# Feed-forward up projections of a two-layer decoder: 18 of 22 column blocks by seven block products, activations kept in three portions

## What is computed

```
y = x * rsqrt(mean(x*x) + 1e-6) * gain
g, u = split(y @ w_gu, 2)            # w_gu: 1024 x (2 * 2816)
x = x + 0.5 * (silu(g) * u) @ w_down # w_down: 2816 x 1024
```

## Time and profile before

| | us |
|---|---|
| median of three runs (2206.16 to 2210.08) | 2208.39 |
| the profiled execution, its own time | 2211.56 |
| its span, first to last instruction | 2209.9 |
| mean granted TensorE clock, share of full | 0.989 |

### The profile page before, as it was taken

The page is one execution under the profiler, slowest core; times in us unless marked ns, Lnnn a source line. Parts: engine busy times, 40 slices in busy tenths (PEclk is TensorE's granted clock), DMA queues, the critical chain, the costliest instruction groups (busy, mean ns, idle before and its releaser), DMA issues.

```text
span 2209.9 us, 32685 instructions
## 1 busy us (share of the span) xinstructions
PE 2150.4 (97%) x12778; PEld 1748.2 (79%) x12778; DVE 1116.6 (51%) x1335; ACT 756.9 (34%) x997; POOL 373.5 (17%) x376
## 2 busy tenths in 40 slices
PE   7999999998988999999999999999999999999998
PEld 6888888776887888888877888887667688888887
DVE  4443445666855544344574433446665654434464
ACT  5432222353323342222353422223444443322234
POOL 2000003444541200000330000013333310000032
PEclk9999999998999999999999999999999999999999
DMA  5324322321002433333243323324323243243232
GB/s 153 95 77 113 95 76 86 87 67 38 4 4 59 124 95 88 103 96 85 88 117 91 90 86 109 95 77 115 86 76 87 65 120 99 78 113 95 74 88 86
DMA packets 365441, 192.35 MB, mean 87 GB/s; under 512 B 10015, under 2 KB 362385, under 8 KB 365345
## 3 DMA queue, kind: packets, MB, share of 16 engines
q1 hardware_dynamic: 363104, 185.10, 29.9%
q0 software_dynamic: 2224, 5.86, 0.9%
q10 hardware_dynamic: 16, 0.00, 0.0%
HBM read 188.81 MB, written 2.13 MB: 86 GB/s over the span
## 4 chain that ended last, share of the span: by engine, by line
PE 91%; DVE 4%; ACT 2%; issue 2%; POOL 1%; DMA 0%; SPq 0%; POOLq 0%; DVEq 0%; ACTq 0%
PE bank L420 25%; PE bank L422 25%; PE bank L421 25%; PE bank L1469 2%; PE bank L2114 2%; PE bank L2116 2%; PE bank L2115 2%; PE bank L831 1%; PE bank L832 1%; PE bank L833 1%; PE bank L2131 1%; PE bank L2150 1%; PE bank L2161 1%; DVE w_lo L410 1%; ACT w_hi L405 0%
## 5 line engine op out<-in xcount | busy, mean ns | idle before, releaser
L420 PE MATMUL bank<-xn_hi,w_hi 128*128 128x512 f32 x1416 | 555.0, 392 | 10.6 <-DVE w_lo L2618 5.8
L421 PE MATMUL bank<-xn_hi,w_lo 128*128 128x512 f32 x1416 | 552.6, 390 | 0.0
L422 PE MATMUL bank<-xn_lo,w_hi 128*128 128x512 f32 x1416 | 552.4, 390 | 0.0
L405 ACT CAST w_hi<-w_raw 128x2048 fp32r<-128x2048 f32 (+3 forms) x209 | 325.7, 1558 | 641.4 <-PE bank L422 560.0
L410 DVE TENSOR_TENSOR w_lo<-w_raw,w_hi 128x2048 fp32r<-128x2048 f32 (+3 forms) x207 | 423.7, 2047 | 148.0 <-ACT w_hi L405 147.2
L420 PEld LDWEIGHTS bank<-xn_hi,w_hi 128*128 128x128 f32 x1416 | 266.7, 188 | 69.2 <-DVE w_lo L2618 6.0
L421 PEld LDWEIGHTS bank<-xn_hi,w_lo 128*128 128x128 f32 x1416 | 266.8, 188 | 56.3 <-issue 1.0
L422 PEld LDWEIGHTS bank<-xn_lo,w_hi 128*128 128x128 f32 x1416 | 266.9, 188 | 55.7
L422 PE MATMUL bank<-h_lo,w_hi 128*128 128x512 f32 x704 | 273.9, 389 | 0.0
L420 PE MATMUL bank<-h_hi,w_hi 128*128 128x512 f32 x704 | 273.9, 389 | 0.0
L421 PE MATMUL bank<-h_hi,w_lo 128*128 128x512 f32 x704 | 273.9, 389 | 0.0
(11 more groups left out here) (337 smaller groups left out, 2682.5 us busy)
## 6 DMA issues: line engine op xcount, KB each, us to landing
w_raw<-in_ffn_w_gu_dram SPq DMA_DIRECT2D x176, 512.0 KB, 5.0
w_raw<-in_ffn_w_down_dram SPq DMA_DIRECT2D x64, 384.0 KB, 3.9
w_raw<-in_ffn_w_down_dram SPq DMA_DIRECT2D x64, 320.0 KB, 3.6
w_raw<-in_even_w_in_dram SPq DMA_DIRECT2D x40, 256.0 KB, 3.3
w_raw<-in_ple_w_gate_dram SPq DMA_DIRECT2D x16, 512.0 KB, 3.8
w_raw<-in_fox_w_in_dram SPq DMA_DIRECT2D x16, 512.0 KB, 4.8
w_raw<-in_even_w_out_dram SPq DMA_DIRECT2D x16, 256.0 KB, 3.3
w_raw<-in_fox_w_in_dram SPq DMA_DIRECT2D x16, 256.0 KB, 4.1
```

The source lines that it names most:

```text
L405: nc.scalar.copy(w_hi[slot][:, 0:tiles], w_raw[slot][:, 0:tiles]).then_inc(w_hi_ready, 1)
L420: nc.tensor.matmul(dst, w[0], hi[:, k], start=k == 0, stop=False)
L421: nc.tensor.matmul(dst, w[1], hi[:, k], start=False, stop=False)
L422: last = nc.tensor.matmul(dst, w[0], lo[:, k], start=False, stop=k == tiles - 1)
```

## The change

**Seven products for eight.** An up job is a product of a matrix of weights, cut into 2x2 pieces (the two halves of the output, gate and other, by the two halves of the 1024 channels), with a matrix of activations, cut into 2x2 pieces (channels 0 to 511 and 512 to 1023, tokens 0 to 255 and 256 to 511). In place of the eight products of pieces the new job makes seven, with sums of pieces as operands (Winograd's arrangement). Each product has 4 blocks of channels, 3 matmuls each, with 256 columns in place of 512: 84 matmuls of 128x256 for 48 of 128x512. It is used for 18 of the 22 up jobs of each feed-forward block, 72 in all; the first 4 (CLASSIC) run as before, and the activation sums are made meanwhile.

**The sums.** Per job GpSimd makes four 128x512 sums or differences of weight pieces (`ffn_pool`; one of them in place in w_raw, three into the single buffer sums), ScalarE rounds those three (`split_sums_hi`, 128x1536) and VectorE makes their low part (`split_sums_lo`). GpSimd starts on the next job only when the low part of the last sums is made (`s_ready`). Per feed-forward block VectorE multiplies x by gain and rinv (`scale_all`, 8 instructions), GpSimd makes four 128x1024 differences of the result, and both, with three 128x1024 pieces of the scaled activations themselves, are split again (`t_his`, `t_los`, `b_hi`, `b_lo`).

**Putting together.** The seven results go to halves of banks; ScalarE copies one (p1, 128x256) and VectorE combines them in five instructions (u2, u4_u3 and three writes to gu). Silu and the product now follow from gu, and the rounding of a job's result stands in the next job.

**Portions.** CHUNKS = (8, 7, 7) takes the place of (12, 10): three sets of up jobs and three sets of 8 down jobs, over 8, 7 and 7 blocks. The up jobs of the first portion are written out, of the others the first is. The core of the diff:

```diff
-HALVES = (12, 10)
+CHUNKS = (8, 7, 7)
+CLASSIC = 4
+T_ORDER = (0, 2, 1, 3)
...
+        p1, u2 = rinv[:, 0:T // 2], rinv[:, T // 2:T]
+        u4_u3 = other
+        at(SCRATCH)
+        gu = view("gu", [P, 2 * T])
+        at(SCRATCH + 8)
+        sums = view("sums", [P, 12, P])
...
-        def each_job(e, name, step, peel_first=False):
+        def each_job(e, name, step, lead=0):
 
 
 
             base, count = jobs.phases[name]
-            lead = 2 if peel_first else 0
             for j in range(lead):
                 step(base + j, j, (base + j) % 2, jobs.of(base + j + 2))
+            if lead == count:
+                return
...
+                    if not isinstance(j, int) or j >= (CLASSIC + 2 if c == 0 else 2):
+                        e.wait_ge(s_ready, seven(st, c, j) - 1)
...
+        def ffn_pool(pool, st):
+            norm, i = norms[st], ffn_index[st]
+            left, right = slice(0, T // 2), slice(T // 2, T)
+
+            def difference(dst, plus, minus):
+                nc.gpsimd.tensor_tensor(t_sum[:, dst], plus, minus, ALU.subtract).then_inc(t_made, 1)
+
+            pool.wait_ge(scaled_made, DT * i + DT // 2)
+            difference(0, scaled_k1[:, :, right], scaled_k1[:, :, left])
+            pool.wait_ge(scaled_made, DT * i + DT)
+            difference(2, scaled_k2[:, :, right], scaled_k1[:, :, right])
+            pool.wait_ge(t_made, 4 * i + 1)
+            difference(1, scaled_k2[:, :, right], t_sum[:, 0])
+            pool.wait_ge(t_made, 4 * i + 3)
+            difference(3, scaled_k2[:, :, left], t_sum[:, 1])
+
+            for c, tiles, h0 in chunks(st):
+                def up(n, j, slot, _):
+                    if classic(c, j):
+                        return
+                    f = seven(st, c, j)
+                    w = w_raw[slot]
+                    pool.wait_ge(w_loaded[slot], loads_due(n, slot))
+                    if not isinstance(j, int) or (c, j) != (0, CLASSIC):
+                        pool.wait_ge(s_ready, f)
+                    nc.gpsimd.tensor_tensor(sums[:, 0:4], w[:, 8:12], w[:, 12:16], ALU.add).then_inc(sums_made, 1)
+                    pool.wait_ge(sums_made, f * 4 + 1)
+                    nc.gpsimd.tensor_tensor(w[:, 8:12], w[:, 0:4], w[:, 8:12], ALU.subtract).then_inc(sums_made, 1)
+                    nc.gpsimd.tensor_tensor(sums[:, 4:8], sums[:, 0:4], w[:, 0:4], ALU.subtract).then_inc(sums_made, 1)
+                    pool.wait_ge(sums_made, f * 4 + 3)
+                    nc.gpsimd.tensor_tensor(sums[:, 8:12], w[:, 4:8], sums[:, 4:8], ALU.subtract).then_inc(sums_made, 1)
+                each_job(pool, f"{st}up{c}", up, tiles if c == 0 else 3)
...
+            def of_seven(dst, w, b):
+                for k in range(4):
+                    nc.tensor.matmul(dst, w[0][:, k], b[0][:, k], start=k == 0, stop=False)
+                    nc.tensor.matmul(dst, w[1][:, k], b[0][:, k], start=False, stop=False)
+                    last = nc.tensor.matmul(dst, w[0][:, k], b[1][:, k], start=False, stop=k == 3)
+                return last
...
+                    pe.wait_ge(w_ready, n + 1)
+                    pe.wait_ge(s_ready, f + 1)
+                    pe.wait_ge(banks_free, n - 1)
+                    if first:
+                        pe.wait_ge(t_ready, 4 * i + 4)
+                    of_seven(bank[2 * slot][:, left], s(0), t(0))
+                    of_seven(bank[2 * slot][:, right], w(8), t(2)).then_inc(parts_done, 1)
+                    if first:
+                        pe.wait_ge(b_ready, 3 * i + 1)
+                    if f_before(f):
+                        pe.wait_ge(u2_made, f)
+                    of_seven(bank[5][:, left], w(0), b(0, left))
+                    of_seven(bank[5][:, right], s(1), t(1)).then_inc(parts_done, 1)
+                    if first:
+                        pe.wait_ge(b_ready, 3 * i + 2)
+                        pe.wait_ge(banks_free, n)
+                    if f_before(f):
+                        pe.wait_ge(c12_made, f)
+                    of_seven(bank[1][:, left], s(2), b(1, right))
+                    of_seven(bank[1][:, right], w(12), t(3)).then_inc(parts_done, 1)
+                    if first:
+                        pe.wait_ge(b_ready, 3 * i + 3)
+                    else:
+                        pe.wait_ge(act_in_ready, j + (g0 + sum(CHUNKS[:c])))
+                    of_seven(bank[3][:, left], w(4), b(1, left)).then_inc(job_done, 1)
+                each_job(pe, f"{st}up{c}", up, tiles if c == 0 else 1)
...
+                def up_classic(n, j, slot, ahead):
+                    act.wait_ge(job_done, n + 1)
+                    if j == CLASSIC - 1:
+                        b_hi(0, scaled_k1, left)
+                        b_hi(1, scaled_k2, right)
+                        gate(j)
+                        split_seven_hi(n + 2, seven(st, c, j + 2), slot)
+                        b_hi(1, scaled_k2, left)
+                        return
+                    if classic(c, j + 2):
+                        split_hi(act, n + 2, slot, ahead)
+                    else:
+                        split_seven_hi(n + 2, seven(st, c, j + 2), slot)
+                    gate(j)
+                    if not classic(c, j + 2):
+                        split_sums_hi(seven(st, c, j + 2), slot)
+                    h_high(j, prod)
+                    if j == 1:
+                        t_his()
...
+                    nc.scalar.copy(p1[:], bank[5][:, left]).then_inc(p1_copied, 1)
+                    if first:
+                        split_sums_hi(f + 1, 1 - slot)
+                        h_high(j - 1, prod)
+
+                    def gate_seven():
+                        act.wait_ge(act_in_ready, j + (g + 1))
+                        act.wait_ge(c12_made, f + 1)
+                        nc.scalar.activation(bank[4][:], gu[:, 0:T], ACT.Silu).then_inc(act_out_ready, 1)
+
                     act.wait_ge(job_done, n + 1)
-                    split_hi(act, n + 2, slot, ahead)
-                    act.wait_ge(act_in_ready, j + (g0 + 1))
-                    nc.scalar.activation(act_out[:], act_in[:], ACT.Silu).then_inc(act_out_ready, 1)
-                    act.wait_ge(prod_ready, j + (h0 + 1))
-                    nc.scalar.copy(h_hi[:, ds(j)], prod[:]).then_inc(h_hi_ready, 1)
-                each_job(act, f"{st}up{half}", up)
-                g0 += tiles
-                h0 += tiles
+                    if last:
+                        gate_seven()
+                        split_hi(act, n + 2, slot, ahead)
+                    elif isinstance(j, int) and j + 2 == tiles:
+                        split_hi(act, n + 2, slot, ahead)
+                        gate_seven()
+                    else:
+                        split_seven_hi(n + 2, f + 2, slot)
+                        gate_seven()
+                        split_sums_hi(f + 2, slot)
+                    h_high(j, bank[6])
+                each_job(act, f"{st}up{c}", up, tiles if c == 0 else 1)
...
+                    if to_up and j == DT - 2:
+                        split_sums_hi(f, slot)
                     act.wait_ge(job_done, n + 1)
-                    split_hi(act, n + 2, slot, ahead)
-                each_job(act, f"{st}down{half}", down)
+                    if to_up:
+                        split_seven_hi(n + 2, f, slot)
+                    else:
+                        split_hi(act, n + 2, slot, ahead)
+                    if to_up and j == DT - 1:
+                        split_sums_hi(f, slot)
+                each_job(act, f"{st}down{c}", down)
...
+                    if first:
+                        b_lo(0, scaled_k1, left, 1)
+                        classic_prod(n - 1, j - 1)
+                        b_lo(1, scaled_k2, right, 2)
+                        split_lo(dve, n + 1, 1 - slot, 2 * DT)
+                        b_lo(1, scaled_k2, left, 3)
+                        split_sums_lo(f + 1, 1 - slot)
+                        dve.wait_ge(prod_ready, j + h0)
+                    dve.wait_ge(p1_copied, f + 1)
+                    nc.vector.tensor_tensor(u2[:], bank[5][:, right], p1[:], ALU.add).then_inc(u2_made, 1)
+                    dve.wait_ge(u2_made, f + 1)
+                    nc.vector.tensor_tensor(halves(u4_u3[:]), halves(bank[2 * slot][:]),
+                                            u2[:].rearrange("p (o t) -> p o t", o=1).broadcast_to([P, 2, T // 2]),
+                                            ALU.add).then_inc(u34_made, 1)
+                    if not begins:
+                        h_low(j - 1, prod if first else bank[6])
+                    dve.wait_ge(u34_made, f + 1)
+                    nc.vector.tensor_tensor(gu[:, T + T // 2:], bank[2 * slot][:, left], u4_u3[:, right],
+                                            ALU.add).then_inc(banks_free, 1)
+                    dve.wait_ge(parts_done, f * 3 + 3)
+                    nc.vector.tensor_tensor(gu[:, T // 2:T + T // 2], bank[1][:], u4_u3[:],
```

(30 more changed lines are left out.)

215 lines of the change are left out of this document (168 added, 47 removed).

## The result

The changed kernel takes 2237.43 us (median of 4 runs, 2233.67 to 2238.28) against 2208.15 for the kernel before. The ratio is 1.013, with a 95% interval from 1.0117 to 1.0143: slower, as forecast, by 29 us where I had 16. The profiled execution's span is 2236.4 us, 26.5 more than before.

What follows compares the result with a forecast made beforehand. TensorE's matmul count and spacing were taken to bound the feed-forward blocks. Terms of - 63 + 51 + 23 + 5 = + 16 us on the median of 2208.4 gave 2224, range 2174 to 2266 (the forecast's own 2213 to 2242).

Steps and rivals of the forecast that it cites:

- Part 1: Matmuls of the 72 new up jobs: 84 narrow ones, 0.1201 us apart or 0.1134; jobs of 10.0 us, 63 us won.
- Part 2: New up jobs: GpSimd's sums and VectorE's work form a loop through the single sums buffer, 10.1 us a job.
- The loop of 10.1 us: New up jobs: two GpSimd sums, ScalarE's rounding, then VectorE's wait, w_lo, product and low part of the sums.
- rival (a): New up jobs: narrow matmuls 0.1134 us apart, loop 9.4, jobs 9.53; 2170 to 2190 us, chance 0.29.
- Part 3: Down to up borders, twice a block: pauses of 3.9 and 5.7 us plus half clock; 12.8 a block, 51 in all.
- Part 4: From old up jobs to new ones: VectorE late with operands, 5.7 us a block, 23 in all.
- I take a pause of 2.4: Before each block's first new job: VectorE's work with port waits takes 35.2 us, TensorE wants it at 32.6.
- Part 5: Up to down borders and the last portion's down jobs: small waits, 1.2 us a block, 5 in all.
- (b): New up jobs: narrow matmuls 0.127 us apart, only 15 us won; 2272 us, chance 0.07.
- (c): New up jobs: GpSimd and VectorE contend for the SBUF port, loop 11.2 us; 2287 us, chance 0.07.
- (d): New up jobs: weight loads and streams add up, 18.3 us a job; 2821 us, chance 0.01.
- (e): Whole kernel: pauses and gain cancel, 2204 to 2213 us, chance 0.11.

Runs made afterwards that it cites:

- Experiment 9: Kernel before, with down-job matmuls cut in columns (four of 128 in the first portion, 384 and 128 in the second), each with its own weight load: 2986.75 us.
- experiment 8: Changed kernel with GpSimd's four weight sums of each job cut to one column, except in each block's first new job (results wrong): 2193.79 us.
- Experiment 2: Changed kernel with weights split before sums for the first up job of the second and third portions: 2214.07 us, ratio 1.0034.
- experiment 7: Changed kernel with five old up jobs a block and VectorE's four t_lo split in two pairs over two jobs: 2210.72 us, ratio 1.0013.
- Experiments 3: Changed kernel with five old up jobs ahead of the new ones in each block, in place of four: 2223.97 us, ratio 1.0075.
- experiment 1: Kernel before, with portions of 8, 7 and 7 in place of 12 and 10, all up jobs as before: 2221.48 us, ratio 1.007.

## Why the prediction came out as it did

**Part 1, right, its size 5 us too good.** The spacing is 0.120, the candidate with a fixed 0.0134 us on 256 columns. Experiment 9 has a third point: 384 columns at 0.173 = 0.160 + 0.013. The forecast took 10.0 us a job, from between 9.53 and 10.1; measured 10.08, 57.6 won and not 63.

The Trainium skill's rule (TensorE: Matmul & The Clock Gate, Part 3, What overlaps and what doesn't), by which loads of the same rows would add to the streams, is not borne out by any run: 0.120 for 256 columns, 0.173 for 384.

**Part 2, right in that GpSimd's work hinders VectorE, wrong in what follows.** The loop of 10.1 us set the pace nowhere but in the two jobs behind the first new one, for 0.2 us a block: TensorE, at 10.08, has no gap in a steady row of jobs, and without the sums (experiment 8) such a row is no faster. How close the loop is can be read in the second portion of the first block, where VectorE's s_lo does not wait for TensorE:

```profile
178.40 1.74 DVE L800 TENSOR_TENSOR s_lo<-sums,s_hi 128x1536 fp32r<-128x1536 f32 x1
...
188.26 1.74 DVE L800 TENSOR_TENSOR s_lo<-sums,s_hi 128x1536 fp32r<-128x1536 f32 x1
```

The loop takes 9.86 us, 0.2 less than TensorE's job, and over five jobs s_lo's lead over TensorE grows from 1.1 to 1.9. A job faster than 9.86, as rival (a) has it, would have needed a shorter loop as well. The port is worse than I had priced it: three VectorE instructions in one job lost 4.9 us, and GpSimd's own are 1.75 to 2.28 beside VectorE's.

The Trainium skill (GPSIMD Engine Reference, Specifications) has VectorE's instructions with two SBUF inputs in contention with GpSimd for the shared interfaces. The trace agrees, with 2.88 us for 0.69; `other`, with one SBUF input, kept its 0.67.

**Part 3, right.** Pauses of 3.9 and 5.7 were forecast, 2.8 and 4.8 measured. At the first border of the first block the chain went as worked out: load issued at 144.30, GpSimd's first sum at 150.01, s_hi at 155.32, w_hi at 156.71. But VectorE's w_lo followed undisturbed (158.64, 2.29), where I had half of a wait for GpSimd's next sums. It was GpSimd that waited, as the two rows below show. That is 0.45 of the 1.1 us between forecast and measurement. Some 0.25 is a slip in the recorded sum (half-way between 19.5 and 20.4, less 16.3, is 3.65 and not 3.9), and 0.4 the chain, which ended at 160.93, 19.1 us behind the fifth down job and not 19.5. The clock took 12 us in place of 12.8. The part is 46, forecast 51. Experiment 2 shows what I did not ask: how much of the pause is order alone. Half of the part was.

```profile
158.74 3.35 POOL L588 TENSOR_TENSOR sums<-w_raw 128x512 f32<-128x512 f32 x1 [3.45 <-DVE s_lo L800]
```

```profile
158.64 2.29 DVE L444 TENSOR_TENSOR w_lo<-w_raw,w_hi 128x2048 fp32r<-128x2048 f32 x1
```

**Part 4, the mis-sized term.** Forecast 23 (ends 8 and 36), measured 37.0, beyond its own upper end: 9.3 a block and not 5.7. The failed step is "I take a pause of 2.4": it was 5.4. I had VectorE's queue right, but GpSimd's hold on the port at four differences of up to 1.95 us, 7.8 in all. It was 11.2 (experiment 7), 3.4 more: the weight sums of the first new job follow the differences without a break, and they hit the t_lo as well. What I had as 3.3 for operands that come late inside the first new job came out at 3.7, but only half of it is that: in experiment 7, where no half clock came, 1.9 a block is left. The rest is the half clock, which I had nowhere in this part. Experiments 3 and 7 show that it is the queue: no instruction was taken out, four were split 2 and 2, and the pause went.

**Part 5, one sentence wrong, and near its number by luck.** "The 32 additional down jobs have VectorE's 0.69 beside the same number of matmuls: nothing." Cutting the down jobs to 7 tiles cost 10 us in experiment 1 and 5.9 in the changed kernel, not for their number but for their length. I had given the third portion up to 0.6 a block for its chain of 4.4 to 4.8 us against 4.76; it is 1.4, because three jobs in it have a hitch and each hitch costs some 0.26 us beside its pause. The 0.3 us that I had at two of three borders from up to down, 2.4 in all, did not come: TensorE has no pause there. So 5.9 for a forecast of 5 is two errors that nearly cancel.

**The rivals.** (a) and (b) fall by the spacing, (c) by experiment 8, (d) by the spacing, (e) by the result. The recorded bounds, 2174 to 2266, do not reach the centres of (b) and (c), 2272 and 2287, though the text says that they leave out only half of (c). My sum for the blocks was 16, the account's is 30.7: 5.4 more in part 1, 14.0 in part 4, 0.9 in part 5, 4.9 less in part 3, and 0.7 less in the first up jobs. The other stages' 4.2 the other way bring the span to + 26.5.

## What to carry to other kernels

A change that removes work from the busiest engine pays only if the chains of the others still fit under its shorter jobs. List, for each border between phases, the chain from the freed buffer to the first operand, with its order on each engine; of 46 us at eight borders, another order alone gave 23 back, and half a load and one sum run ahead gave 32. Spread one-time preparation over jobs instead of queueing it behind one; the queue hits the next thing behind it, whatever that is. And look at what the half clock adds behind each pause: in experiment 2 the eight pauses got 13 us shorter (30.3 to 17.2) and the time 23. Last, read how much lead the second slowest engine has inside a row of jobs: here it was 0.2 us a job, so faster matmuls alone would soon have won nothing.

## What the runs showed of the hardware that I had not expected

A 128-column matmul with its own 128x128 load comes every 0.111 us, the same as loads with hardly anything to multiply: the load sets it. At half clock it is 0.213. 256 columns at 0.120 are 0.009 above this floor, so that cutting columns further than the changed kernel does would win next to nothing.

Matmuls of 128 columns ran at half clock for 238.8 us in which TensorE had no gap; a pause of 1.71 us stood 1.5 us ahead of this stretch. In rows of matmuls with 256 columns the clock was 1.00. So a low clock that lasts is no sign of pauses while it lasts.

GpSimd and VectorE stretch each other in both directions: VectorE's 512-column product of two SBUF tensors took 2.88 in place of 0.69 us, and GpSimd's sum of 512 columns 3.35 in place of 1.29 beside a w_lo of 2.29. In that last pair w_lo had started 0.10 us earlier and kept its length; the sum ended 1.16 us behind it (162.09 and 160.93).
